# Stick attention with v as the stationary operand, memory projections spread between all heads, and the ends of the blocks in another order

## The chip, the cores and the metric

The kernel runs on one core of a Trainium2 chip as one launch. The metric is the device time of the launch in microseconds (us). TensorE (PE) multiplies, VectorE (DVE) and ScalarE (ACT) do the elementwise work, GpSimd (POOL) does almost nothing here, and SyncE (SP) starts the weight loads. Each engine runs its own list of instructions in order; semaphores order them against each other.

## What is computed

Two transformer blocks stand behind each other. The first one has a gated FFN, a mixer of two attentions, and a second gated FFN. The second one has two layers; this change concerns it above all:

```
# layer 0: latent attention (8 heads, a value width of 128)
lat = h @ w_dkv; c_q, c_kv = rmsnorm(lat[:384]), rmsnorm(lat[384:640])
q = c_q @ w_uq; k, v = c_kv @ w_ukv; softmax(q k^T + causal) v  @ w_o
# layer 1: stick attention (8 heads of 128)
z = q k^T * scale; log_fail = where(strict, -softplus(z), 0)
excl = cumsum(log_fail, reverse) - log_fail
a = where(strict, exp(log_sigmoid(z) + excl), 0);  o = a v  @ w_o
# after either: cross attention to 256 memory rows (4 heads), then square(relu(h w)) w
```

There are S = 256 rows of width 1024, kept as two tiles t of 128 rows. The memory's keys and values are `rmsnorm(mem) @ w_kv`; they do not depend on the layers before them.

## The kernel before

Every weight product is made three times, from float32r halves: `mm3` multiplies high by high, high by low, low by high (lines 377 to 379, of 512 columns mostly). The weights come as chunks of up to 4 tiles of 128x512, in the fixed order of `PLAN`. A chunk passes three stations: a load by SP into the ring `w_raw`, its high part by ACT (`split_hi`, L349), its low part by DVE (`split_lo`, L357). The ring has 4 slots. So where PE has finished chunk n, ACT and DVE split chunk n+4 (`next_hi`, `next_lo`). The place of `next_hi(n)` and `next_lo(n)` in the lists of ACT and DVE is written by hand in each phase. Whatever stands behind a split there waits for it.

Phases follow each other on each engine. What the prediction speaks of:

- `Ffn` steps. At a step, PE multiplies, ACT applies the activation (`take_up_scalar`, L653 or L656), DVE makes the product or the square (`hide_vector`, L715 or L719). At the end, `residual_vector` (L485) adds the result to h, in two halves of 512 columns; `norm_tensor` (L411) turns h on PE, `norm_scalar` (L421) and `norm_vector` (L467) take its high and low parts as `xt_h`, `xt_l`; `rms_scalar` (L430) and `root_vector` (L445 to L454) make the root mean squares, which are needed only where products are copied out of PSUM. `tail_scalar` and `tail_vector` set this order: three of the four splits, the first half of the norm, a split, the second half, and only then the phase `Norm` with the squares and the root.
- `Project` copies products out (`copy_out`, L927, with the row's factor from `rs`), turns them on PE (L884), and takes them. For 8x64 heads DVE makes a norm between (`squares`, L996; `normalise`, L1007). `mla_down` makes the two latents, `mla_up` multiplies them up.
- `Fill` is a projection of the memory, keys or values, in steps placed between the groups of an attention: 0 to 3 are 12 matmuls each, 2 and 7 also the splits, 4 the copy (L1144), 5 the turning and 6 the taking of keys (L1132, L1151).
- `Attend` for latent attention: in groups, scores (L1244), logits (L1339), exponential (L1319), turning of the probabilities (L1253), values (L1264); and `Finish`, which makes rows of the result (L1191), turns them (L1203) and takes them (L1210, L1216).
- `Stick`, one head at a time (g = 0 to 7): scores (L1546), mask on DVE (L1619), three functions on ACT (L1597 to L1599), softplus on DVE (L1629), suffix sums on PE (L1556 to L1558), their sum on DVE (L1625), the exponential on ACT (L1605), and the value product with the weights a as the stationary and v as the moving operand:

```
nc.tensor.matmul(bankD[0][g // 4][:, c], a[:, 0:P], vals[0], start=True, stop=True)
nc.tensor.matmul(bankD[1][g // 4][:, c], a[:, P:S], vals[0], start=True, stop=False)
nc.tensor.matmul(bankD[1][g // 4][:, c], a[:, S:S + P], vals[1], start=False,
                 stop=True).then_inc(self.summed, 1)
```

  This gives rows of o, so that `Finish` has to copy and turn them (L1197, L1203) before the output projection can use them. After every fourth head two tiles are finished.
- `OutProject` is the output projection; its tail is again `tail_scalar` and `tail_vector`.

## Time and profile before

| | before |
|---|---|
| median of 3 runs | 1339.06 us (1335.96 to 1339.08) |
| the profiled execution's own time | 1339.2 us |
| span of its trace | 1337.4 us |
| PE, DVE, ACT busy | 1277.5, 760.9, 649.4 us |
| mean granted TensorE clock | 0.992 |

The span runs from the first to the last instruction of the trace; 1.8 us of the time lie outside it. PE is busy for 96% of the span. Matmuls are pipelined and their ends are modelled, so an unbroken row of matmuls counts as busy throughout. A granted clock of 1.00 is 2.4 GHz, one of 0.50 is 1.2 GHz.

### The profile page before, as it was taken

Reading aid. Unit: us, or ns where it says so; the run is one execution under the profiler, and the core shown is the slowest. Engines: PE = TensorE matmul, PEld = TensorE weight load, DVE = VectorE, ACT = ScalarE, POOL = GpSimd, SP = SyncE. Lnnn points to the kernel's source line nnn. Section 1 sums busy time; section 2 is a strip of 40 time slices with the busy share of each in tenths; the row PEclk is TensorE's granted clock in tenths of the full one; section 3 lists DMA queues with packets and bytes.
Section 4 is the critical chain, followed back from the end, with each engine's and each line's share of the span. In section 5 each row is a group of like instructions: output and inputs, shape, how many; then the busy total and the mean of one; then the engine's idle time right before and its main releaser. Section 6 shows DMA issues by size and latency. Waiting matters only on the chain.

```text
span 1337.4 us, 16848 instructions
## 1 busy us (share of the span) xinstructions
PE 1277.5 (96%) x6786; PEld 1089.5 (81%) x6786; DVE 760.9 (57%) x1075; ACT 649.4 (49%) x828; POOL 11.9 (1%) x16
## 2 busy tenths in 40 slices
PE   6999998999999999997999999999999899999996
PEld 4888887888887888887888789999787777889895
DVE  6554448787675555547645475554644546654544
ACT  5444436464355454446844464443645645543432
POOL 0000000001000000000000000000000000000000
PEclk9999999999999999999999999999999899999998
DMA  6855545554444555545623265554554122555530
GB/s 248 283 188 188 187 142 209 189 173 134 166 148 149 185 188 187 189 137 171 210 73 111 79 235 185 184 190 144 212 188 169 69 95 88 208 197 190 188 124 32
DMA packets 38685, 221.72 MB, mean 166 GB/s; under 512 B 4533, under 2 KB 4549, under 8 KB 23120
## 3 DMA queue, kind: packets, MB, share of 16 engines
q1 hardware_dynamic: 36256, 214.26, 46.4%
q0 software_dynamic: 912, 3.75, 0.8%
q10 hardware_dynamic: 1440, 2.64, 0.8%
q8 instruction: 54, 0.88, 0.3%
q14 instruction: 23, 0.19, 0.0%
HBM read 219.55 MB, written 1.07 MB: 165 GB/s over the span
## 4 chain that ended last, share of the span: by engine, by line
PE 86%; DVE 6%; ACT 5%; issue 2%; DMA 1%; DVEq 0%; SPq 0%; ACTq 0%
PE ps L377 22%; PE ps L379 22%; PE ps L378 22%; PE ps L573 4%; PE ps L575 4%; PE ps L574 4%; DVE wlo L357 3%; PE ps L1244 2%; ACT whi L349 2%; PE ps L1264 2%; PE ps L411 1%; PE ps L884 1%; PE ps L1253 1%; PE ps L606 1%; ACT xt_h L421 1%
## 5 line engine op out<-in xcount | busy, mean ns | idle before, releaser
L357 DVE TENSOR_TENSOR wlo<-w_raw,whi 128x2048 fp32r<-128x2048 f32 (+4 forms) x245 | 470.2, 1924 | 415.9 <-ACT whi L349 415.5
L349 ACT ACTIVATE whi<-w_raw 128x2048 fp32r<-128x2048 f32 (+4 forms) x245 | 394.7, 1616 | 449.4 <-PE ps L379 344.5
L377 PE MATMUL ps<-whi,xt_h 128*128 128x512 f32 (+3 forms) x784 | 309.6, 395 | 11.6 <-DVE wlo L357 4.0
L379 PE MATMUL ps<-whi,xt_l 128*128 128x512 f32 (+3 forms) x784 | 304.2, 388 | 0.0
L378 PE MATMUL ps<-wlo,xt_h 128*128 128x512 f32 (+3 forms) x784 | 303.7, 387 | 0.0
L377 PE MATMUL ps<-whi,ot_h 128*128 128x512 f32 x594 | 235.9, 397 | 5.6 <-ACT nat L927 3.6
L379 PE MATMUL ps<-whi,ot_l 128*128 128x512 f32 x594 | 232.2, 391 | 0.0
L378 PE MATMUL ps<-wlo,ot_h 128*128 128x512 f32 x594 | 231.9, 390 | 0.0
L377 PEld LDWEIGHTS ps<-whi,xt_h 128*128 128x128 f32 x784 | 148.5, 189 | 46.4 <-issue 13.3
L379 PEld LDWEIGHTS ps<-whi,xt_l 128*128 128x128 f32 x784 | 148.3, 189 | 30.0
L378 PEld LDWEIGHTS ps<-wlo,xt_h 128*128 128x128 f32 x784 | 148.4, 189 | 27.5
L573 PE MATMUL ps<-xt_h,whi 128*128 128x256 f32 x512 | 145.3, 284 | 3.2 <-DVE xt_l L467 1.8
L574 PE MATMUL ps<-xt_h,wlo 128*128 128x256 f32 x512 | 144.9, 283 | 0.0
L575 PE MATMUL ps<-xt_l,whi 128*128 128x256 f32 x512 | 144.9, 283 | 0.0
L377 PEld LDWEIGHTS ps<-whi,ot_h 128*128 128x128 f32 x594 | 111.9, 188 | 28.8 <-issue 6.2
L379 PEld LDWEIGHTS ps<-whi,ot_l 128*128 128x128 f32 x594 | 111.8, 188 | 24.1
L378 PEld LDWEIGHTS ps<-wlo,ot_h 128*128 128x128 f32 x594 | 112.0, 189 | 21.7
L573 PEld LDWEIGHTS ps<-xt_h,whi 128*128 128x128 f32 x512 | 98.2, 192 | 4.9 <-issue 4.4
L574 PEld LDWEIGHTS ps<-xt_h,wlo 128*128 128x128 f32 x512 | 98.2, 192 | 0.5
L575 PEld LDWEIGHTS ps<-xt_l,whi 128*128 128x128 f32 x512 | 98.2, 192 | 0.0
L421 ACT ACTIVATE xt_h<-ps,gain 128x256 fp32r<-128x256 f32 x88 | 34.3, 479 | 49.4 <-PE ps L411 49.4
L467 DVE SCALAR_TENSOR_TENSOR xt_l<-ps,gain,xt_h 128x256 fp32r<-128x256 f32 x88 | 36.3, 477 | 23.0 <-ACT xt_h L421 23.0
(185 smaller groups left out, 871.6 us busy)
## 6 DMA issues: line engine op xcount, KB each, us to landing
w_raw<-ffn_mid SPq DMA_DIRECT2D x80, 768.0 KB, 4.3
w_raw<-mlp_mid SPq DMA_DIRECT2D x56, 1024.0 KB, 4.9
w_raw<-w_qkv SPq DMA_DIRECT2D x12, 1024.0 KB, 4.9
w_raw<-w_sb_qkv SPq DMA_DIRECT2D x12, 1024.0 KB, 4.8
w_raw<-w_xkv SPq DMA_DIRECT2D x8, 1024.0 KB, 4.8
w_raw<-ffn_first SPq DMA_DIRECT2D x8, 512.0 KB, 4.9
w_raw<-w_gate_b SPq DMA_DIRECT2D x4, 1024.0 KB, 5.0
w_raw<-w_gate_a SPq DMA_DIRECT2D x4, 1024.0 KB, 4.9
```

Of the source, the lines that this page charges most:

```text
L349: nc.scalar.activation(whi[:, s, 0:tiles * width], w_raw[:, s, 0:tiles * width], ACT.Copy).then_inc(w_hi, 1)
L357: nc.vector.tensor_tensor(wlo[:, s, 0:tiles * width], w_raw[:, s, 0:tiles * width], whi[:, s, 0:tiles * width].bitcast(F32), ALU.subtract) ...
L377: nc.tensor.matmul(acc, hi, whi[:, s, c], start=start, stop=False)
L378: nc.tensor.matmul(acc, hi, wlo[:, s, c], start=False, stop=False)
L379: return nc.tensor.matmul(acc, lo, whi[:, s, c], start=False, stop=stop)
L421: last = nc.scalar.activation(to[:, k], bank[:, j * S:(j + 1) * S], ACT.Copy, scale=gain[:, 8 * NORM[name] + k:8 * NORM[name] + k + 1])
L467: last = nc.vector.scalar_tensor_tensor(out=lo[:, k], in0=bank[:, j * S:(j + 1) * S], scalar=g, in1=hi[:, k].bitcast(F32), op0=ALU.mult, o ...
L573: nc.tensor.matmul(acc, whi[:, s, c], xt_h[:, k], start=k == 0, stop=False)
L574: nc.tensor.matmul(acc, wlo[:, s, c], xt_h[:, k], start=False, stop=False)
L575: last = nc.tensor.matmul(acc, whi[:, s, c], xt_l[:, k], start=False, stop=k == KC - 1)
L1244: last = nc.tensor.matmul(bankA[g % 2][:, head["at"]:head["at"] + head["width"]], q, k, start=i == 0, stop=i == len(head["qk"]) - 1)
L1264: last = nc.tensor.matmul(head["out"], pt[:, g % 2, c:c + P], val, start=i == 0, stop=i == len(head["v"]) - 1)
```

## The change

It has these parts, all of which leave the arithmetic as it is, except that the sums of some roots are made in two instructions' rows instead of one.

1. `Ffn`: at the start only one chunk is split ahead of the first activation instead of two. At the end DVE adds the residual first; the order is then a split, half of the norm, a split, the other half, squares and root, and then the last two splits.
2. `mla_down` and `mla_up`: the root for the query latent is made in a row of instructions of its own, ahead of the one for the key latent; `mla_up` waits for `mla_down`'s copies tile by tile.
3. Latent attention: heads are grouped in their own order, so that results can be finished after every fourth head. The memory's values come first and begin before the first scores (step -1); the keys come behind them, and their turning is placed in the output projection.
4. Stick attention: v is the stationary operand, so the result comes turned and goes from PSUM straight to `ot_h` and `ot_l`, a pair of heads at a time. There is no `Finish`. The memory's values, then its keys, stand between all heads.

```diff
-        for part in ("keys", "values"):
+        for part in ("values", "keys"):
             add(f"mem_{part}{i}", f"w_xkv{i}", [4] * 2)
...
@@ Ffn.scalar
-                for c in range(2):
-                    next_hi(act, self.n0 + c)
+                next_hi(act, self.n0)
                 act.wait_ge(rs_ready, RMS_AT[self.name])
                 self.take_up_scalar(act, 0)
-                for c in range(2, 4):
+                for c in range(1, 4):
                     next_hi(act, self.n0 + c)
...
-                tail_scalar(act, [self.n0 + 4 * self.steps + c for c in range(4)], self.following)
+                chunks = [self.n0 + 4 * self.steps + c for c in range(4)]
+                for half, n in enumerate(chunks[:2]):
+                    next_hi(act, n)
+                    if self.following:
+                        norm_scalar(act, self.following, half)
+                if self.following:
+                    rms_scalar(act, self.following)
+                for n in chunks[2:]:
+                    next_hi(act, n)
@@ Ffn.vector
-                for c in range(2):
-                    next_lo(dve, self.n0 + c)
+                next_lo(dve, self.n0)
                 self.hide_vector(dve, 0)
-                for c in range(2, 4):
+                for c in range(1, 4):
                     next_lo(dve, self.n0 + c)
...
+                for half, n in enumerate(chunks[:2]):
+                    residual_vector(dve, self.down_full, self.scale, half)
+                    next_lo(dve, n)
+                    if self.following:
+                        norm_vector(dve, self.following, half)
+                if self.following:
+                    root_vector(dve, self.following)
+                for n in chunks[2:]:
+                    next_lo(dve, n)
@@ Project
+                            if part and part[0] == unit.ks[0] and unit.u == 0 and self.before:
+                                pe.wait_ge(self.before.evac, NT * (len(self.before.units) - 1) + t + 1)
...
+                if unit.u == 3 and self.before:
+                    act.wait_ge(self.before.rooted, 2)
...
+            def root(self, dve, unit):
+
+                c = 2 * len(NORMS) + 2 * unit.u
+                dve.wait_ge(self.squared, unit.u + 1)
+                rsqrt(dve, ms[:, c:c + 2], rs[:, c:c + 2], 1.0, EPS, 2).then_inc(self.rooted, 1)
...
+                    if unit.kind == "latent":
+                        self.root(dve, unit)
...
@@ Attend.tensor and Stick.tensor
+                for filler, step in fill_steps(self.fillers, -1):
+                    filler.tensor(pe, step)
                 for s, value in self.need:
                     pe.wait_ge(s, value)
@@ Stick
+            def pair_bank(self, pair):
+                return bankD[0][pair % 2]
+
             def value(self, pe, g):
+
                 pe.wait_ge(self.weights, g + 1)
-                if g in self.bank_free:
-                    pe.wait_ge(*self.bank_free[g])
...
+                if g >= 4:
+                    pe.wait_ge(self.lo, g // 2 - 1)
...
-                nc.tensor.matmul(bankD[0][g // 4][:, c], a[:, 0:P], vals[0], start=True, stop=True)
-                nc.tensor.matmul(bankD[1][g // 4][:, c], a[:, P:S], vals[0], start=True, stop=False)
-                nc.tensor.matmul(bankD[1][g // 4][:, c], a[:, S:S + P], vals[1], start=False,
+                nc.tensor.matmul(bank[:, at:at + S], vals[0], a[:, 0:S], start=True, stop=False)
+                nc.tensor.matmul(bank[:, at + P:at + S], vals[1], a[:, S:S + P], start=False,
                                  stop=True).then_inc(self.summed, 1)
 
+            def take_hi(self, act, pair):
+                act.wait_ge(self.summed, 2 * pair + 2)
+                nc.scalar.activation(ot_h[:, 2 * pair:2 * pair + 2],
+                                     self.pair_bank(pair).rearrange("p (k s) -> p k s", k=2), ACT.Copy)\
+                    .then_inc(self.hi, 1)
...
@@ Stick.vector (Stick.scalar likewise)
                     for filler, step in fill_steps(self.fillers, g):
                         filler.vector(dve, step)
-                    for f in range(4):
-                        if self.fin.fins[f][2] == g - 1:
-                            self.fin.out_rows(dve, f)
-                        if self.fin.fins[f][2] == g - 2:
-                            self.fin.take_lo(dve, f)
+                    if g >= 3 and g % 2:
+                        self.take_lo(dve, g // 2 - 1)
@@ OutProject.tensor
+                    if c == 0 and self.aside:
+                        self.aside.tensor(pe, 5)
@@ mla_groups
-                for heads in same_half(per):
+                for heads in [list(range(h0, h0 + per)) for h0 in range(0, 8, per)]:
@@ the phases
+        values0 = memory_values(0, bankD[1], (-1, 0, 1, 2, 2, None, None, 3))
+        keys0 = memory_keys(0, bankD[0], [(rows_lo, rows0 + 1), (rows_lo, rows0 + 2)], 1,
+                            (4, 5, 6, 7, 7, None, None, 8), bankT)
...
+        values1 = memory_values(1, bankD[1], (-1, 0, 1, 2, 2, None, None, 3))
+        keys1 = memory_keys(1, bankD[1], [(fill_copied, values1.full0 + 1), (fill_copied, values1.full0 + 2)], 0,
+                            (3, 4, 5, 6, 6, 7, 7, 7))
+        stick = Stick("sb", [sb_in.turned_ready, sb_in.evac_ready], (values1, keys1))
+        sb_out = OutProject("sb_out", "sb_o", all8, ot_h, ot_l, [(stick.lo, 3), keys1.ready],
+                            following="cross1", need_k={6: (stick.lo, 4)})
```

The programs were laid beside each other at three places. The first is ACT's list at the end of the first FFN; L349 is a split, L421 (L419 after) the norm, L430 (L428) the squares, L927 (L944) the copy of the next phase's first product. Before:

```order
L349 ACTIVATE whi<-w_raw 128x2048 x2
L349 ACTIVATE whi<-w_raw 128x1296
L421 ACTIVATE xt_h<-ps,gain 128x256 x4
L349 ACTIVATE whi<-w_raw 128x1296
L421 ACTIVATE xt_h<-ps,gain 128x256 x4
L430 ACTIVATE lg,ms<-h 128x1024 x2
L349 ACTIVATE whi<-w_raw 128x2048
L927 ACTIVATE nat<-ps,rs 128x512 x2
```

And after:

```order
L349 ACTIVATE whi<-w_raw 128x2048
L419 ACTIVATE xt_h<-ps,gain 128x256 x4
L349 ACTIVATE whi<-w_raw 128x2048
L419 ACTIVATE xt_h<-ps,gain 128x256 x4
L428 ACTIVATE lg,ms<-h 128x1024 x2
L349 ACTIVATE whi<-w_raw 128x1296 x2
L349 ACTIVATE whi<-w_raw 128x2048
L944 ACTIVATE nat<-ps,rs 128x512 x2
```

Two splits have moved from ahead of the norm to behind the squares, so that three splits now stand between the squares and the first copy, where one stood. DVE's list has moved in the same way.

The second place is PE's list where latent attention begins, behind the last product of `mla_up`. Before:

```order
L378 MATMUL ps<-wlo,ot_h 128x512
L379 MATMUL ps<-whi,ot_l 128x512
L1244 MATMUL ps<-kt,qt 128x128
L1244 MATMUL ps<-pet 128x128
L1244 MATMUL ps<-kt,qt 128x128
```

And after:

```order
L378 MATMUL ps<-wlo,ot_h 128x512
L379 MATMUL ps<-whi,ot_l 128x512
L377 MATMUL ps<-whi,xt_h 128x512
L378 MATMUL ps<-wlo,xt_h 128x512
L379 MATMUL ps<-whi,xt_l 128x512
```

Twelve matmuls of the memory's values (the first three are shown) now stand ahead of the first scores.

The third place is DVE's list at the end of stick attention: L1619 (L1659 after) is the mask, L1625 (L1665) the sum of logits and suffix sums, L1629 (L1669) softplus, L1216 (L1609) the low part of the result. Before:

```order
L1619 TENSOR_TENSOR lg<-ps,const 128x384
L1625 TENSOR_TENSOR lg<-lg,ps 128x384
L1629 SCALAR_TENSOR_TENSOR pt<-lg,pt 128x384
L1625 TENSOR_TENSOR lg<-lg,ps 128x384
L357 TENSOR_TENSOR wlo<-w_raw,whi 128x2048
L1197 COPY nat<-ps 128x512 x2
L1216 TENSOR_TENSOR ot_l<-ps,ot_h 128x4x128 x2
```

And after:

```order
L1659 TENSOR_TENSOR lg<-ps,const 128x384
L1665 TENSOR_TENSOR lg<-lg,ps 128x384
L1669 SCALAR_TENSOR_TENSOR pt<-lg,pt 128x384
L357 TENSOR_TENSOR wlo<-w_raw,whi 128x2048
L1609 TENSOR_TENSOR ot_l<-ps,ot_h 128x512
L1665 TENSOR_TENSOR lg<-lg,ps 128x384
L1609 TENSOR_TENSOR ot_l<-ps,ot_h 128x512
```

The copies of rows are gone, and a split and a low part now stand ahead of the last head's sum, where they stood behind it.

## Rows read from the trace of the kernel before

**Rows 1.** The page: the engines' busy times; a weight load, its size and landing

```profile
PE 1277.5 (96%) x6786; PEld 1089.5 (81%) x6786; DVE 760.9 (57%) x1075; ACT 649.4 (49%) x828; POOL 11.9 (1%) x16
...
w_raw<-w_qkv SPq DMA_DIRECT2D x12, 1024.0 KB, 4.9
```

**Rows 2.** Stretches: length, busy PE, PEld, DVE, ACT, POOL, then PE's clock, DMA

```profile
66.80:100.20 33.40, 33.40 (x153) 27.64 (x152) 16.96 (x15) 14.77 (x14) 0.00 (x0) 1.00 0.56 188
...
199.00:231.00 32.00, 27.45 (x139) 22.89 (x138) 25.92 (x49) 21.16 (x29) 0.00 (x0) 0.95 0.54 188
422.00:435.00 13.00, 10.94 (x43) 8.59 (x42) 8.33 (x12) 7.82 (x8) 0.00 (x0) 0.87 0.62 207
600.00:634.20 34.20, 26.96 (x158) 24.19 (x157) 26.68 (x70) 23.83 (x48) 0.00 (x0) 1.00 0.54 181
658.50:709.00 50.50, 46.03 (x264) 39.14 (x264) 25.83 (x55) 25.38 (x53) 0.00 (x0) 1.00 0.35 122
946.00:970.00 24.00, 22.29 (x106) 18.03 (x105) 19.33 (x30) 15.96 (x19) 0.00 (x0) 1.00 0.65 233
1026.50:1084.00 57.50, 48.78 (x255) 40.63 (x254) 29.88 (x44) 33.98 (x54) 0.00 (x0) 0.94 0.24 85
```

**Rows 3.** PE at the first FFN's end: start, length, instruction, idle before

```profile
205.81 1.29 PE L411 MATMUL ps<-const,h 128*128 128x128 f32 x8 [2.96 <-DVE h L485]
```

**Rows 4.** DVE from there to the next phase's first norm

```profile
202.18 2.29 DVE L357 TENSOR_TENSOR wlo<-w_raw,whi 128x2048 fp32r<-128x2048 f32 x1 [1.95 <-ACT whi L349]
204.39 1.28 DVE L485 SCALAR_TENSOR_TENSOR h<-ps,h 128x512 f32<-128x512 f32 x2
...
217.53 0.17 DVE L445 TENSOR_SCALAR ms<-ms 128x2 f32<-128x2 f32 x1 [1.29 <-ACT lg L430]
...
229.78 1.29 DVE L1007 TENSOR_TENSOR nat<-nat,hs 128x512 f32<-128x512 f32 x2
```

**Rows 5.** ACT over the same stretch

```profile
217.41 1.90 ACT L349 ACTIVATE whi<-w_raw 128x2048 fp32r<-128x2048 f32 x1
221.33 0.69 ACT L927 ACTIVATE nat<-ps,rs 128x512 f32<-128x512 f32 x1 [2.02 <-PE ps L379]
```

**Rows 6.** The starts of the FFNs: PE in the first, DVE and PE in the second

```profile
29.98 0.47 PE L377 MATMUL ps<-whi,xt_h 128*128 128x512 f32 x1 [1.07 <-DVE nat L715]
...
423.42 3.43 DVE L357 TENSOR_TENSOR wlo<-w_raw,whi 128x1536 fp32r<-128x1536 f32 x2 [0.53 <-ACT whi L349]
426.77 0.87 DVE L715 SCALAR_TENSOR_TENSOR nat<-ps,rs,lg 128x256 f32<-128x256 f32 x2
...
427.39 0.47 PE L377 MATMUL ps<-whi,xt_h 128*128 128x512 f32 x1 [2.06 <-DVE nat L715]
```

**Rows 7.** PE in the latent projections

```profile
626.25 0.47 PE L377 MATMUL ps<-whi,ot_h 128*128 128x512 f32 x1 [0.88 <-ACT nat L927]
...
633.97 0.47 PE L377 MATMUL ps<-whi,ot_h 128*128 128x512 f32 x1 [2.71 <-ACT nat L927]
```

**Rows 8.** PE in latent attention: its start, and the output projection's start

```profile
661.37 0.46 PE L1244 MATMUL ps<-kt,qt 128*128 128x128 f32 x2 [1.50 <-ACT v L918]
...
708.60 0.47 PE L377 MATMUL ps<-whi,ot_h 128*128 128x512 f32 x1 [0.82 <-issue]
```

**Rows 9.** ACT behind the first MLP: the stick projection's first copy

```profile
965.71 0.69 ACT L927 ACTIVATE nat<-ps,rs 128x512 f32<-128x512 f32 x1 [1.74 <-PE ps L379]
```

**Rows 10.** Stick attention: PE after head 3 and at the end, then ACT

```profile
1058.93 1.46 PE L1203 MATMUL ps<-const,nat 128*128 128x128 f32 x8 [2.73 <-DVE nat L1197]
...
1078.22 1.25 PE L1203 MATMUL ps<-const,nat 128*128 128x128 f32 x8 [1.55 <-DVE nat L1197]
...
1083.05 0.47 PE L377 MATMUL ps<-whi,ot_h 128*128 128x512 f32 x1 [0.82 <-issue]
...
1059.97 0.52 ACT L1597 ACTIVATE pt<-lg 128x384 f32<-128x384 f32 x1 [4.02 <-DVE lg L1619]
...
1061.60 0.51 ACT L1605 ACTIVATE nat<-lg 128x384 f32<-128x384 f32 x1
```

More of the change, by code:

```diff
@@ L382, in norm_banks @@
         def norm_banks(name):
[L385 removed]
+            if name.startswith("mem"):
                 return bankD[1] + bankD[0]
[L387 to L388 removed]
             return bankT + bankD[0]
@@ L1114, in tensor @@
                         pe.wait_ge(xt_lo, 4 * NORM[self.normed] + 2 * (c + 1))
-                    if step == 0:
-                        for s, value in self.free:
+                    if c == 0:
+                        for s, value in self.free[t:t + 1]:
                             pe.wait_ge(s, value)
@@ L1575, in tensor @@
                 self.score(pe, 0)
-                for g in range(H2 + 3):
+                for g in range(H2 + 1):
                     if g + 1 < H2:
```

119 lines of the change are left out of this document (59 added, 60 removed).

## The prediction

> **What bounds the kernel.** I read the page first. PE is busy for 1277.5 of 1337.4 us, the others for 57% and less [rows 1]. In a dense stretch it has no gap: 153 matmuls in 33.40 us, 0.22 each [rows 2]. So an edit pays only by removing PE work or PE's waits, 59.9 us in all. The stretches that the change touches hold half of the waits: length less PE's busy time is 4.55, 2.06, 7.24, 4.47, 1.71 and 8.72 us, 28.8 together [rows 2]. The rest is in the start, the cross attentions and the end, which stay. In three of those stretches the clock was also granted at half rate for a while: a mean of 0.95 over 32 us is 3.2 us at 1.2 GHz, 0.87 over 13 is 3.4, 0.94 over 57.5 is 6.9 [rows 2]. A 3.4 us spell costs 1.7 us of dense work. Such spells came in the stretches with waits of 2.96, 2.06 and 2.73 us [rows 3, 6, 10], none in the one with a wait of 2.71 [rows 2, 7].
>
> My method is to carry the new order through: each instruction keeps its duration from the trace and starts when its engine is free and its inputs are there. What counts is by how much PE's next unavoidable point comes earlier, not the wait that is removed.
>
> **Starts of the FFNs.** PE waits 1.07 us for the product of step 0 [rows 6]; and since a matmul behind a wait counts 0.47 long [rows 6] where the pace is 0.22 [rows 2], a wait also costs part of that difference, for which I take 0.16. With one split ahead instead of two the product comes 1.7 earlier, half of the pair that takes 3.43 [rows 6]: the first FFN gains 1.2. In the second, ACT's activation then starts as soon as the product of tile 0 is full, DVE's split ends at 425.1, its product at 425.5, and PE goes on at 425.6 instead of 427.39 [rows 6]: 1.75, and the half-clock spell should go with the wait, 1.7 more. Cover for the split that is now later: the first chunk of the step, 18 matmuls or about 4 us, against 3.1 for its two parts. In the MLPs nothing is gained: there DVE's root ends after the activation, and the first split stands behind it in either order.
>
> **End of the first FFN.** DVE splits (202.18, 2.29) before it adds the residual (204.39), and PE waits 2.96 until 205.81 [rows 3, 4]. PE stopped at 202.85, one chunk of 6 matmuls beyond what the residual needs. So in the new order the residual can start at about 201.0 and ends at 202.3, before PE gets there, and PE turns h at once and begins the next projection at 205.3, 4.9 earlier. But two splits now stand behind the squares. ACT: squares end at 212.4 (217.4 less 5.0), two splits of 1296 columns (1.2 each) and one of 2048 (1.9) follow, and the copy that stood at 221.33 [rows 5] starts at 216.7; PE wants it at 217.05, a wait of 0.3. DVE: root at 212.5 (217.53 less 5.0); from there to the normalise it took 12.25, of which 0.33 idle [rows 4], and two splits of 1.4 come in between: 227.3 instead of 229.78, only 2.5 earlier. PE reaches the turn that needs it at 224.5 and waits 3.4. So the gain is 2.5, and a wait of 3.4 us on DVE's L1007 stands where the one on L485 stood. It is longer than the one that brought the clock down before, so I charge 1.7 for a spell.
>
> **End of the second FFN and the latents.** The same way PE begins `mla_down` 3.8 earlier. Three splits ahead of the first copy give 1.7 back as a wait. Then the root of the query latent, a row of twelve small instructions that starts with one like that of 217.53 [rows 4] and takes 2.3 in the trace, stands ahead of DVE's `lower` and `rotate`: `mla_up` starts at 624.75 instead of 626.25, with a wait of 2.2 in place of 0.88 [rows 7]. The wait of 2.71 for the copy behind it [rows 7] is not ended by the root at all: ACT first takes the key latent, which PE has just turned, and that order stays. It moves with PE, to 2.9. Net gain 1.6.
>
> **Latent attention.** The values' first 12 matmuls (2.7 us) cover the wait of 1.50 for the last copy of v; the output projection no longer waits 0.82 for the copy of the bank [rows 8], since a bank is copied while the other one fills; the finishes (the rest of the 4.47 [rows 2]) now have a fill step behind each. Followed through, one wait of 0.35 stays, at the second finish. PE's work is the same: 96 fill matmuls, the same scores, turns and values. Gain 4.1, and 0.16 for each of five waits: 5.0.
>
> **End of the first MLP.** PE begins the stick projection 1.9 earlier. But ACT's squares, moved by as much, end at 960.1, three splits of 1.9 follow, and the copy of 965.71 [rows 9] comes at 965.8 all the same. PE waits 1.7 and the gain is 0.2.
>
> **Stick attention.** The value product keeps its 384 moving columns per head (three matmuls of 128 before, one of 256 and one of 128 now). What goes are 16 transposes, 8 of them in 1.46 at half clock or 0.87 at full [rows 10], so 1.7 us, and the waits for the copied rows, 2.73 and 1.55 [rows 10]. The start gains nothing: the first values step waits about 1.5 for `xt_l`, which the scores used to cover, and the first softplus is late anyway, because DVE's last split of the projection stands ahead of the first mask. Through head 2 all stays. Then splits (DVE 2.29, ACT 1.90 [rows 4, 5]) stand in the steps of heads 3, 5 and 7, each followed by a pair's two parts (0.6 and 0.65), and behind them the next mask, three functions (1.64 from 1059.97 to 1061.60 [rows 10]) and softplus. I get the suffix products of heads 4, 6 and 7 at 1056.0, 1066.5 and 1069.9, with waits of 0.7 to 1.0. The last head is the sore point: DVE's sum for it now stands behind a split and a low part. ACT takes the keys and splits until 1072.6, DVE until 1075.4, the sum ends at 1075.9, the exponential at 1076.5, while PE is done with head 6 at 1071.4: a wait of 5.1 us in front of the last value product. The output projection starts at 1077.25 instead of 1083.05 [rows 10]: gain 5.8. One spell behind the 5.1 us wait costs 1.7; the 6.9 us of before are in the 1083.05 already.
>
> **Sum.** 1.2 + 3.5 + 2.5 + 1.6 + 5.0 + 0.2 + 5.8 = 19.8, less 3.4 for two spells, 16.4. From the profiled execution's 1339.2, which is the median of the runs within 0.2, this gives 1322.8.
>
> **A rule weighed.** The trace shows spells in the stretches of the waits of 2.96, 2.06 and 2.73, but a clock of 1.00 through the one with 2.71 and 0.88 [rows 2, 7]. The Trainium skill, in TensorE: Matmul & The Clock Gate, section What's actually happening, says that the low rate is the default and activity lifts it; by that rule each of my new waits may bring a spell, and the time would be that of the third case below.
>
> **Rivals.**
> 1. As worked out: 1318 to 1327, chance 0.50.
> 2. The splits aren't in the way as I think, because the engines catch up. Then the ends of the three blocks give 4.9, 4.0 and 1.9 instead of 2.5, 1.6 and 0.2 (6.5 more), the 5.1 wait goes and both spells (3.4): 15 more, 1308. Range 1303 to 1318. Against it: DVE was idle for only 6.1 us of the 32 at the first FFN's end [rows 2]. Chance 0.16.
> 3. The clock falls more often: the two new waits of 2.2 and 2.9 in the latents bring a spell each and stick attention a second one, 1.7 each: 1328. Up to 1332. For it: the 6.9 us behind one wait of 2.73. Chance 0.20.
> 4. The attentions aren't shortened. They alternate between four engines, and if each hand-over takes the slack, 5.0 and 5.8 shrink to the transposes' 1.7: 1332. For it: DVE and ACT were idle for nearly half of these stretches (29.88 and 33.98 busy of 57.5 [rows 2]), so it is latency that sets them; against it: PE had work in most gaps. Chance 0.08.
> 5. Slower. Two splits later at three block ends also means that the loads into their slots start later, since SP waits for both parts of the split. If the weights of four chunks later came late, PE would stand. At the first FFN's end the split ends at 216.4 instead of 209.3; the load (4.9 [rows 1]) and the next split (1.9 and 2.3) end at 226, and PE wants that chunk behind two more products, after 239. It decides only if loads take 13 us longer, and for a slower kernel 5.5 us more at each of three places. Chance 0.04.
>
> The remaining 0.02 is for gains and losses that cancel. A measurement of this kernel tells 0.3%, some 4 us, from no change. Cases 1 to 4 all end below 1335: faster 0.94, same 0.02, slower 0.04. The range 1312 to 1332 leaves out the better half of case 2 and the tails of 3 and 4, about 2 in 10.
>
> **What would show it.** In the new profile: no PE wait on the residual at the ends of the FFNs; instead waits of about 3.4 on the normalise, 1.7 on the first copies, 2.2 and 2.9 in the latents; 0.3 at the second FFN's start with the clock at 1.00; at most 0.5 of waits in latent attention; one wait of about 5 in front of the last head's values. If PE's busy time falls by more than the 2 us of the transposes and the spells, I have misread the swap. The likeliest error is in the waits of a few us that I worked out over chains of ten or more instructions.

## The result and the profile after

The changed kernel took 1324.18 us (median of 4 runs, 1322.03 to 1325.89) and the kernel before, measured beside it, 1337.53. The ratio is 0.9892, with a 95% interval from 0.9867 to 0.9917. A second measurement gave 1323.26 us and a ratio of 0.9894 [0.9881, 0.9908]. The gain is real, about 14 us by the ratios and 13.3 by the medians, where the forecast had 16.4. The time of 1324.2 lies 1.4 above the forecast of 1322.8.

The page of the changed kernel, PE's line, answers to [rows 1]:

```profile
PE 1273.8 (96%) x6754; PEld 1088.0 (82%) x6754; DVE 760.2 (57%) x1083; ACT 648.3 (49%) x828; POOL 11.9 (1%) x16
```

The span fell from 1337.4 to 1324.1 us, 13.3. PE's busy time fell by 3.7, so waits of PE make up the other 9.6. The same stretches as in [rows 2], moved by about as much as PE came earlier there (columns: stretch, length, busy PE, PEld, DVE, ACT, POOL, clock, DMA):

```profile
198.00:227.90 29.90, 26.38 (x141) 22.39 (x140) 26.26 (x49) 22.25 (x30) 0.00 (x0) 0.99 0.58 204
418.40:429.80 11.40, 11.01 (x51) 8.81 (x50) 9.05 (x18) 9.58 (x11) 0.00 (x0) 1.00 0.34 107
592.70:630.90 38.20, 32.12 (x173) 28.49 (x172) 29.61 (x84) 26.11 (x50) 0.00 (x0) 0.95 0.48 162
655.20:700.10 44.90, 43.95 (x257) 38.37 (x256) 25.23 (x54) 22.99 (x49) 0.00 (x0) 1.00 0.39 133
...
1017.80:1069.20 51.40, 43.73 (x221) 36.14 (x220) 28.80 (x40) 34.29 (x54) 0.00 (x0) 0.98 0.32 113
```

Length less busy PE is the waits: 0.39 at the second FFN's start (2.06 before), 0.95 in latent attention (4.47 before), but 7.67 in stick attention (8.72 before), and 6.08 in the latents. So stick attention got shorter by 6.1 us with only 1.05 us less of waits in it; what fell there is PE's busy time, by 5.05. About 2 us of that is the clock and not work: the half-clock spell of before, 6.8 us long, lies in its stretch whole, while the new one starts at 1067.2 and this stretch ends at 1069.2. The 16 transposes were 2.3 us: from their first start to the start of what follows, eight took 1.25 from 1058.93 on and eight 1.01 from 1078.22 on.

PE's own rows say which waits those are. They are nearly the new ones of the forecast:

```profile
29.02 0.47 PE L377 MATMUL ps<-whi,xt_h 128*128 128x512 f32 x1
...
227.05 1.72 PE L899 MATMUL ps<-const,nat 128*128 128x128 f32 x8 [3.15 <-DVE nat L1024]
228.42 0.78 PE L377 MATMUL ps<-whi,xt_h 128*128 128x512 f32 x1
...
423.82 0.47 PE L377 MATMUL ps<-whi,xt_h 128*128 128x512 f32 x1 [0.39 <-DVE nat L721]
...
610.00 0.38 PE L377 MATMUL ps<-whi,xt_h 128*128 128x320 f32 x1 [1.46 <-ACT nat L944]
619.74 0.53 PE L377 MATMUL ps<-whi,ot_h 128*128 128x512 f32 x1 [1.80 <-DVE ot_l L1066]
629.10 0.47 PE L377 MATMUL ps<-whi,ot_h 128*128 128x512 f32 x1 [2.71 <-ACT nat L944]
...
682.16 0.66 PE L1227 MATMUL ps<-const,nat 128*128 128x128 f32 x4 [0.95 <-DVE nat L1215]
...
958.01 0.47 PE L377 MATMUL ps<-whi,xt_h 128*128 128x512 f32 x1 [1.31 <-ACT nat L944]
...
1019.50 0.50 PE L377 MATMUL ps<-whi,xt_h 128*128 128x512 f32 x1 [1.46 <-DVE xt_l L465]
1026.96 0.70 PE L1581 MATMUL ps<-pt,const 128*128 128x256 f32 x2 [0.36 <-DVE pt L1669]
...
1067.06 1.09 PE L1597 MATMUL ps<-nat,v 128*128 128x256 f32 x2 [4.74 <-ACT nat L1646]
1067.94 0.63 PE L1598 MATMUL ps<-nat,v 128*128 128x128 f32 x2
1068.23 0.77 PE L377 MATMUL ps<-whi,ot_h 128*128 128x512 f32 x1
1068.80 0.63 PE L378 MATMUL ps<-wlo,ot_h 128*128 128x512 f32 x1
```

A spell here is a stretch in which the granted clock is 0.50. A matmul of 512 columns in an unbroken row shows 0.63 us there instead of 0.4. The trace's clock record has four spells of 3.4 us each ahead of the last ten us in the changed kernel, at 227.5, 620.1, 630.3 and 1067.2 us, at most 1.2 us behind the ends of the waits of 3.15, 1.80, 2.71 and 4.74. Before it had three, at 206.5, 428.4 and (6.8 us, twice as long as each of the others) 1059.8. The profiled execution of the changed kernel is the slowest of its four (1325.89 us).

By how much does the same matmul of PE come earlier? The table takes the matmul of the same ordinal at each place. "Behind the spell" is a matmul a few us later, where a spell that one of the two kernels has there is over.

| place | before | after | earlier by |
|---|---|---|---|
| first FFN, step 0's product | 29.98 | 29.02 | 0.96 |
| behind the turn of the normed heads | 231.54 | 228.42 | 3.12, and 1.96 behind the spell at 227.5 |
| second FFN, step 0's product | 427.39 | 423.82 | 3.57, and 5.15 behind before's spell |
| `mla_up` | 626.25 | 619.74 | 6.51, and 3.29 behind the spells at 620.1 and 630.3 |
| latent attention's output projection | 708.60 | 699.70 | 8.90, soon 8.11 |
| stick projection, behind its first wait | 966.81 | 958.01 | 8.80 |
| stick attention's output projection | 1083.05 | 1068.23 | 14.82, and 13.70 behind the spell at 1067.2 |
| end of the span | 1337.4 | 1324.1 | 13.3 |

### The profile page after: what moved, and what is told of

It is laid out like the page before. It is cut to its first block, busy times and chain, and to the rows that moved or that the text cites. A ratio compares the mean times of both kernels' runs of the same rounds, so it can differ in the third digit from the quotient of the medians.

```text
span 1324.1 us, 16795 instructions
## 1 busy us (share of the span) xinstructions
PE 1273.8 (96%) x6754; PEld 1088.0 (82%) x6754; DVE 760.2 (57%) x1083; ACT 648.3 (49%) x828; POOL 11.9 (1%) x16
## 3 DMA queue, kind: packets, MB, share of 16 engines
HBM read 219.55 MB, written 1.07 MB: 167 GB/s over the span
## 4 chain that ended last, share of the span: by engine, by line
PE 86%; DVE 7%; ACT 5%; issue 2%; DMA 0%; DVEq 0%; SPq 0%; ACTq 0%
PE ps L377 22%; PE ps L379 22%; PE ps L378 22%; PE ps L572 4%; PE ps L574 4%; PE ps L573 4%; DVE wlo L357 3%; PE ps L1268 2%; PE ps L1288 2%; ACT whi L349 2%; PE ps L899 1%; PE ps L409 1%; PE ps L1277 1%; ACT xt_h L419 1%; PE ps L605 1%
## 5 line engine op out<-in xcount | busy, mean ns | idle before, releaser
L349 ACT ACTIVATE whi<-w_raw 128x2048 fp32r<-128x2048 f32 (+4 forms) x245 | 394.5, 1616 | 433.6 <-PE ps L379 329.7
L419 ACT ACTIVATE xt_h<-ps,gain 128x256 fp32r<-128x256 f32 x88 | 34.3, 479 | 52.1 <-PE ps L409 52.1
```

The lines of the kernel that those rows point to most:

```text
L349: nc.scalar.activation(whi[:, s, 0:tiles * width], w_raw[:, s, 0:tiles * width], ACT.Copy).then_inc(w_hi, 1)
L419: last = nc.scalar.activation(to[:, k], bank[:, j * S:(j + 1) * S], ACT.Copy, scale=gain[:, 8 * NORM[name] + k:8 * NORM[name] + k + 1])
```

## The experiments

All ratios are to the kernel before, each measured beside it on the same chip; the kernel before took 1338.5 to 1338.7 us there. Gains in us are worked out from the ratios.

**The same kernel again.** Nothing is edited; its profile shows the same instructions a second time.

> The changed kernel once more, as the reference for the runs beside it. 0.989 of the kernel before, about 1324 us; half-clock spells at other places than before are likely, each worth 1.7 us.

It took 1323.26 us (1322.56 to 1325.87), 0.9894 [0.9881, 0.9908]. The waits are the same, the clock isn't. Its stretches:

```profile
198.00:229.50 31.50, 27.98 (x144) 24.02 (x143) 28.40 (x50) 23.04 (x30) 0.00 (x0) 0.95 0.62 217
592.70:627.50 34.80, 28.72 (x166) 25.84 (x165) 28.82 (x83) 25.22 (x49) 0.00 (x0) 1.00 0.53 178
1017.80:1069.20 51.40, 45.21 (x219) 37.42 (x218) 26.16 (x33) 30.21 (x47) 0.00 (x0) 0.93 0.29 103
```

and PE's rows in the latents:

```profile
618.63 0.50 PE L377 MATMUL ps<-whi,ot_h 128*128 128x512 f32 x1 [1.80 <-DVE ot_l L1066]
626.38 0.47 PE L377 MATMUL ps<-whi,ot_h 128*128 128x512 f32 x1 [2.71 <-ACT nat L944]
```

The waits of 1.80 and 2.71 are there again, yet the latents ran at a clock of 1.00, with no spell, where the first profile had two; between the two rows lie 7.75 us here and 9.36 there. In stick attention it is the other way round: the spell behind the last values' wait is 6.8 us long here (from 1062.1) and 3.4 in the first profile. The means of 0.93 and 0.98 exaggerate this, as the stretch ends inside the first profile's spell. Against [rows 7], PE is here at both rows 7.6 us earlier than before; in the first profile it was 6.51 and then 4.87 earlier. So the spells of this stretch come in one execution of a kernel and not in another, and cost what a row of dense matmuls loses at half the clock. Those behind the waits of 3.15 and 4.74 are in both profiles (here at 225.9 and 1062.1).

**FFN starts alone.** The kernel before with only this edit, and the same on DVE:

```diff
-                for c in range(2):
-                    next_hi(act, self.n0 + c)
+                next_hi(act, self.n0)
                 act.wait_ge(rs_ready, RMS_AT[self.name])
                 self.take_up_scalar(act, 0)
-                for c in range(2, 4):
+                for c in range(1, 4):
```

> The kernel before with one edit alone: at the start of each FFN one chunk is split ahead of the first activation instead of two. My theory: PE's wait of 1.07 us in the first FFN goes, the one of 2.06 in the second shrinks to about 0.4 and the half-clock spell behind it (1.7 us) goes, the MLPs stay as they are; 4.7 us less than before, about 1333. Rival: the spell stays somewhere else, then 3.0 less. Rival: the later splits are missed by PE a chunk later, then no gain at all.

1336.46 us against 1338.69, ratio 0.9980 [0.9970, 0.9991], which is 2.7 us less: the first rival, not the 4.7 of the theory. The wait of 1.07 is gone, that of 2.06 is 0.39, and the stretch has its full clock:

```profile
420.00:433.00 13.00, 12.61 (x58) 10.11 (x57) 10.23 (x19) 10.45 (x11) 0.00 (x0) 1.00 0.41 130
598.00:637.40 39.40, 33.43 (x176) 29.11 (x175) 27.51 (x71) 24.92 (x50) 0.00 (x0) 0.91 0.52 174
```

But the latents, untouched, ran at 0.91 here and at 1.00 before [rows 2]. This profile has spells at 205.6 (6.8 us), 601.5 and 632.3 that the profile before does not have, or has at half the length, and it is of the slowest of 11 executions (1338.39 us, clock 0.989; the fastest had 1333.76 and 0.993). Over the 11 the mean granted clock is 0.9914, over the 22 of the kernel before 0.9918, so on the whole the 1.7 for the spell that the edit removes was paid again elsewhere. The waits' 2.7 to 3.0 us are what the edit is sure of.

**The ends undone.** The changed kernel with the old order at the ends of the FFNs and of the first MLP (residual behind the third split, the squares and the root in a phase of their own):

```diff
-                chunks = [self.n0 + 4 * self.steps + c for c in range(4)]
-                for half, n in enumerate(chunks[:2]):
-                    residual_vector(dve, self.down_full, self.scale, half)
-                    next_lo(dve, n)
...
+                tail_vector(dve, [self.n0 + 4 * self.steps + c for c in range(4)], self.following,
+                            self.down_full, self.scale)
```

> The changed kernel with the old order at the ends of the FFNs (three splits, norm, split, norm, then squares and root); all else as changed. My theory: the ends gave only 2.5 + 1.6 + 0.2 = 4.3 us in waits and cost half-clock spells in return (three of them, 227.5, 620.1 and 630.3, stand in the changed kernel's trace, one at 206.5 in that of before), so that undoing them costs between 0 and 3 us: 1324 to 1327. PE should wait about 3 us on the residual at the first FFN's end again, and not on L1024. Rival: the ends gave what their removed waits promise, 4.9 + 4.0 + 1.9 = 10.8 us; then about 1335.

1326.96 us, 0.9917 [0.9900, 0.9935]; the changed kernel's ratio is 0.9892 to 0.9894, so the new ends are worth about 3 us. That is at the upper end of what was expected, and the intervals overlap a little. PE's rows at the first FFN's end:

```profile
204.81 1.06 PE L409 MATMUL ps<-const,h 128*128 128x128 f32 x8 [2.96 <-DVE h L483]
209.21 0.47 PE L377 MATMUL ps<-whi,xt_h 128*128 128x512 f32 x1 [1.94 <-DVE xt_l L465]
231.05 1.15 PE L883 MATMUL ps<-const,nat 128*128 128x128 f32 x7 [1.02 <-DVE nat L1008]
```

5.9 us of waits here, against 0.29 (on `xt_l`) and 3.15 in the changed kernel. The difference of 2.5 us is as large as the gain that the prediction worked out for this end.

**Stick part alone.** The kernel before with the new `Stick` and, in layer 1, the values and then the keys between all heads:

```diff
-        stick = Stick("sb", [sb_in.turned_ready, sb_in.evac_ready], fills1, {4: fills1[0].ready})
-        sb_out = OutProject("sb_out", "sb_o", all8, ot_h, ot_l, [stick.ready, fills1[1].ready],
-                            following="cross1")
+        stick = Stick("sb", [sb_in.turned_ready, sb_in.evac_ready], (values1, keys1))
+        sb_out = OutProject("sb_out", "sb_o", all8, ot_h, ot_l, [(stick.lo, 3), keys1.ready],
+                            following="cross1", need_k={6: (stick.lo, 4)})
```

> The kernel before with the stick part alone: v stationary, result taken in pairs straight from PSUM, the memory's values and keys of the second layer in the new places. My theory: the output projection behind stick attention starts 5.8 us earlier relative to its start, one half-clock spell behind the wait of about 4.7 in front of the last values costs 1.6 of it: 4.2 less than before, about 1333.3. Rival: the swap pays by its matmuls and transposes alone, 1.7 us. Rival: no spell, 5.8 less.

1334.98 us, 0.9976 [0.9966, 0.9986], 3.2 us less by the ratio, where 4.2 were expected. The wait in front of the last values is there (4.73 us at 1077.13, L1571 on ACT's L1620).

**The swap without the new places.** The same, but with the memory's keys in the steps of heads 0 to 5 and its values behind head 6, as before:

```diff
-                       (-1, 0, 1, 2, 2, None, None, 3))
...
-                     lambda t: nat[:, 0, t], [], row("mem0"), (3, 4, 5, 6, 6, 7, 7, 7), rel[:, 0:4])
+        keys1 = Fill("mem_keys1", bankD[1], [], lambda t: nat[:, 0, t], [(mem_root.rooted, 1)], row("mem0"),
+                     (0, 0, 1, 2, 2, 3, 3, 5), rel[:, 0:4])
...
+                       lambda t: mem_v[:, t], [], row("mem0"), (7, 8, 9, 10, 11, None, None, 11))
```

> The kernel before with v as the stationary operand in stick attention and the pairs' copies to ot_h and ot_l, but with the memory's keys and then its values where they stood: keys in the steps of heads 0 to 5, values behind head 6, so the values' products cover the end of the last heads. My theory: the swap takes away the rows' copies with the waits of 2.73 and 1.55 in front of their turning, and 1.7 of transposes, and leaves waits on softplus in the heads without a fill; together about 5, so 1332 to 1335 where the kernel before takes 1338.7, as much as the stick part with moved fills gave. Rival A, the new places of the fills are what counts and the swap gives only the transposes: 1337. Rival B, the moved fills cost more (the split ahead of the last sum) than they give: then this kernel is clearly better than the stick part with moved fills, at 1331 or less.

1338.05 us against 1338.47, 0.9994 [0.9986, 1.0003]: nothing that can be told. My theory (about 5 us) was wrong, and rival B too; rival A, the places count, comes nearest in time, though not even the 1.7 of the transposes is left. Two things took the gain back, longer waits and the clock. PE's rows:

```profile
1034.80 0.70 PE L1555 MATMUL ps<-pt,const 128*128 128x256 f32 x2 [1.71 <-DVE pt L1643]
1052.49 1.22 PE L1555 MATMUL ps<-pt,const 128*128 128x256 f32 x2 [2.46 <-DVE pt L1643]
1063.31 1.22 PE L1555 MATMUL ps<-pt,const 128*128 128x256 f32 x2 [4.69 <-DVE pt L1643]
```

and DVE's ahead of the third:

```profile
1057.55 2.29 DVE L357 TENSOR_TENSOR wlo<-w_raw,whi 128x2048 fp32r<-128x2048 f32 x1 [1.92 <-ACT whi L349]
1059.76 0.68 DVE L1583 TENSOR_TENSOR ot_l<-ps,ot_h 128x512 fp32r<-128x512 f32 x1
1060.36 0.55 DVE L1633 TENSOR_TENSOR lg<-ps,const 128x384 f32<-128x384 f32 x1
1060.83 0.55 DVE L1639 TENSOR_TENSOR lg<-lg,ps 128x384 f32<-128x384 f32 x1
1062.70 0.56 DVE L1643 SCALAR_TENSOR_TENSOR pt<-lg,pt 128x384 f32<-128x384 f32 x1 [1.33 <-ACT pt L1614]
```

The waits of 2.73 and 1.55 on the copied rows are gone, and the softplus waits took their place: 2.46 where there had been 0.64 and less, and 4.69 where there had been 0.68, because the next head's mask (L1633) stands behind a split (2.29) and a low part, and ACT's three functions and the softplus come behind the mask. (Ahead of the 2.46 it stands behind a low part alone, which waited 1.41 for its high part.) All six waits of stick attention together were 7.7 us before (1.71, 0.64, 0.37, 2.73, 0.68, 1.55) and are 8.9 here, so 1.2 us of what the transposes gave is lost again. It is the chain of one head that sets the pace at these places, mask to functions to softplus to suffix sums, and part of the time for turning the rows had only filled it.

The other part is the clock. Stick attention's stretch shows

```profile
1020.00:1083.50 63.50, 53.54 (x258) 44.86 (x257) 29.50 (x41) 37.78 (x59) 0.00 (x0) 0.92 0.26 91
```

which is 10.2 us at half the clock, in two spells that start within the waits of 2.46 and 4.69, where the kernel before has 6.8. It is not only this profile: the mean granted clock of the 11 executions is 0.9907 (0.989 to 0.994), that of the 15 of the kernel before 0.9921, and 0.0014 of 1337 us are 1.9 us. So at an equal clock the swap would have given about 2.3 to 2.7 us, an estimate from these means and the 0.4 to 0.8 us of the times. With the new places of the memory's products (the stick part alone) the mean granted clock is 0.9916 again.

**Both attention parts alone.** The kernel before with both attention parts and the separate root for the query latent, without the starts and ends of the FFNs:

> The kernel before with both attention parts and the separate root of the query latent, without the new starts and ends of the FFNs. My theory: 4.8 from latent attention and about 3.7 to 6 from stick attention, as far as a half-clock spell takes some of it back: 1328 to 1330 where the kernel before takes 1338.7. Rival, the attentions give back what they gain and the ends of the blocks make most of the change's gain: 1333 or more.

1330.12 us against 1338.47, 0.9941 [0.9929, 0.9954], 7.9 us less. Of these the stick part is 3.2, so 4.7 are left for latent attention and the root, where the table above has 4.8. Its own profile agrees: against the kernel before, PE is 0.1 us later at the first matmul of `mla_up` (626.35 for 626.25) and 4.7 earlier behind latent attention (709.48 for 714.16). The three groups of parts alone give 2.7, 3 and 7.9, together 13.6 of the 14.2 to 14.4 of the whole change.

**No fill ahead of the first scores.** One number of the changed kernel:

```diff
-        values0 = memory_values(0, bankD[1], (-1, 0, 1, 2, 2, None, None, 3))
+        values0 = memory_values(0, bankD[1], (0, 0, 1, 2, 2, None, None, 3))
```

> The changed kernel, but in latent attention the first step of the memory's values stands behind the first scores, not ahead of them. In the trace of before PE waited 1.50 there for the last copy of v. My theory, that this step covers that wait: about 1.5 longer than the changed kernel, 1325 to 1326 against 1323.3 to 1324.2, and the wait of 1.5 is back in PE's rows. Rival, the slack moves on: the step is then missing ahead of the scores but covers a wait of the same size a group later, and the time stays within 0.5.

1324.23 us, 0.9902 [0.9886, 0.9918]. The time can't tell 1.5 from nothing: the ratios differ by 0.0008 to 0.001, about 1.2 us, and the intervals overlap. The profile can:

```profile
656.68 0.46 PE L1268 MATMUL ps<-kt,qt 128*128 128x128 f32 x2 [1.50 <-ACT v L935]
682.51 0.65 PE L1227 MATMUL ps<-const,nat 128*128 128x128 f32 x4 [0.95 <-DVE nat L1215]
```

The wait of 1.50 of before is back, and the next one, 0.95, is what it is in the changed kernel, so nothing later was covered in its stead. Laid beside the first profile of the changed kernel, PE is 1.40 us earlier at the end of `mla_up` (a spell less there) and 0.36 later at the first matmul of `mla_out`, with no spell between. So latent attention takes 1.76 us longer without the early step, and the rival is out.

**The last sum ahead of the last split.** The 4.74 us wait was worked out as DVE's sum standing behind a split. The edit puts that split, of the keys' second chunk, behind the last head:

```diff
-                            (3, 4, 5, 6, 6, 7, 7, 7))
+                            (3, 4, 5, 6, 6, 7, 7, 8))
```

> The changed kernel with one number changed: the last split of the memory's keys in stick attention stands in step 8 instead of 7, so that DVE makes the last head's sum ahead of that split. My theory: the wait of 4.74 us in front of the last values is the split on ACT (1.9) and the one on DVE (2.3) less what overlaps; it shrinks to about 1.5, a gain of 3.2, and the half-clock spell behind it goes too, 1.6 more: about 1319.5. Rival: the split only moves in front of the output projection's own second chunk, and the gain is given back: 1324. Rival: the spell comes anyway: 1321.

1316.83 us, 0.9843 [0.9827, 0.9859], some 6.6 us less than the changed kernel, where 4.8 were expected. DVE in the changed kernel:

```profile
1063.09 2.29 DVE L357 TENSOR_TENSOR wlo<-w_raw,whi 128x2048 fp32r<-128x2048 f32 x1 [2.62 <-ACT whi L349]
1065.30 0.68 DVE L1609 TENSOR_TENSOR ot_l<-ps,ot_h 128x512 fp32r<-128x512 f32 x1
1065.90 0.55 DVE L1665 TENSOR_TENSOR lg<-lg,ps 128x384 f32<-128x384 f32 x1
```

and in this one:

```profile
1057.70 0.69 DVE L1609 TENSOR_TENSOR ot_l<-ps,ot_h 128x512 fp32r<-128x512 f32 x1 [1.31 <-ACT ot_h L1603]
1058.31 0.54 DVE L1665 TENSOR_TENSOR lg<-lg,ps 128x384 f32<-128x384 f32 x1
1061.24 2.29 DVE L357 TENSOR_TENSOR wlo<-w_raw,whi 128x2048 fp32r<-128x2048 f32 x1 [2.39 <-ACT whi L349]
```

PE's wait there:

```profile
1059.46 0.70 PE L1597 MATMUL ps<-nat,v 128*128 128x256 f32 x2 [1.22 <-ACT nat L1646]
```

The wait fell by 3.5. The clock record has no spell at this place any more: 3.4 us at half the clock in the first profile of the changed kernel, 6.8 in the second. Against the second, which has the same clock up to here, PE is 3.5 us earlier at this matmul and 6.3 behind the spell. So a little over half of the 6.6 is the wait and the rest is the clock.

**First copy and normalise ahead of the splits, and the latents.** Two edits of the changed kernel, each alone. The first puts, in a projection's first unit, ACT's copy ahead of the split that stood before it, and DVE's normalise ahead of the last split:

```diff
+                    if first:
+                        next_lo(dve, unit.n[0][0])
+                        self.normalise(dve, unit)
...
-                    if unit.kind == "qk":
+                    if unit.kind == "qk" and not first:
```

> The changed kernel, with the first copy of the phase behind an FFN ahead of ACT's third split, and on DVE, behind the first FFN, the squares ahead of the splits of the next product's two chunks and the normalise ahead of the second of them. My theory: the wait of 3.15 us on the normalise shrinks to about 1.2, the 1.31 at the stick projection and most of the 1.46 in the latents go; the second of these only moves into the wait behind it. 2 + 1.4 = 3.4 us less than the changed kernel, and the half-clock spell behind the 3.15 may go (1.7 more): 1319 to 1321. Rival: the splits are late for PE in their new place (at the second chunk of the next product), and nothing is gained.

1318.89 us, 0.9855 [0.9837, 0.9873], 5.2 less than the changed kernel. PE's row at the first FFN's end:

```profile
224.71 1.26 PE L899 MATMUL ps<-const,nat 128*128 128x128 f32 x8 [1.28 <-DVE nat L1029]
```

The wait on the normalise is 1.28 instead of 3.15 and no spell follows it. The first copy's 1.31 at the stick projection is gone. In the latents its 1.46 became one of 1.02 on a split's low part, and 2.71 stands in front of `mla_up` where 1.80 did. The second edit makes the root of the query latent behind DVE's `lower`, and ACT takes the last latent behind the first copy of `mla_up`:

```diff
                     if before is not None and before.kind in ("latent", "dkv"):
                         self.lower(dve, before)
+                    if before is not None and before.kind == "latent":
+                        self.root(dve, before)
...
+                    if unit.u == 0 and self.before:
+                        self.before.take(act, self.before.units[-1])
```

> The changed kernel, with the root of the query latent behind its lower part on DVE, and the first copy of the up projection ahead of the taking of the key latent on ACT. My theory: the wait of 1.80 on the lower part becomes a few tenths, the one of 2.71 on the copy goes: 4.3 us less, and the two half-clock spells around them (620.1 and 630.3) go as well, 3.4 more: 1316.5 to 1320. Rival: the copy itself has then to wait for the root, so that only one of the two waits pays: 1321.5. Rival: spells come elsewhere: 1320.

1319.15 us, 0.9855 [0.9841, 0.9868], 5.2 less as well. The wait of 2.71 is gone, the 1.80 is 0.82, and its profile has no spell in the latents:

```profile
618.10 0.50 PE L377 MATMUL ps<-whi,ot_h 128*128 128x512 f32 x1 [0.82 <-DVE ot_l L1068]
```

**All three together.** The last three edits in one kernel:

> The changed kernel with the three edits together: the last head's sum ahead of the last split, the first copies ahead of the third split, and the order in the latents. My theory: the waits that go are different ones and add up: 3.5 + 3.4 + 4.3 = 11 us, and of the four half-clock spells inside the changed kernel at most one stays, up to 5 more: 1309 to 1313. Rival: the engines behind are the bound and each edit uses the same slack; then about 1316, as with the best of the three alone.

1310.00 us (1308.18 to 1310.21), 0.9785 [0.9772, 0.9798]: 28.7 us less than the kernel before, twice what the change brought. By the ratios the three edits alone give 6.6, 5.2 and 5.2, and 14.6 together, 2.4 less than their sum. Its own page has PE busy for 1267.6 of 1308.1 us. Its stretches (end of the first FFN, latents, stick attention):

```profile
198.00:226.00 28.00, 26.43 (x144) 22.75 (x144) 24.93 (x48) 21.85 (x29) 0.00 (x0) 1.00 0.55 189
590.00:625.00 35.00, 31.86 (x174) 28.41 (x173) 28.77 (x83) 25.34 (x50) 0.00 (x0) 0.95 0.52 177
1010.00:1057.00 47.00, 44.35 (x228) 36.87 (x227) 26.08 (x34) 31.20 (x48) 0.00 (x0) 1.00 0.26 90
```

The waits are 1.6, 3.1 and 2.7 us there (the last stretch leaves out the wait of 1.46 on `xt_l` at 1008.7; with it 4.1, against 7.67 in the changed kernel), and only the latents still have a spell.

## Why the prediction was right, and where it was off

**Direction, size and places** were right. The waits came where they were put, and nearly as long: 3.15 on the normalise (3.4 worked out), 0.39 at the second FFN's start (0.3), 1.46 and 1.31 on first copies (1.7 each), 1.80 and 2.71 in the latents (2.2 and 2.9), 1.46 on `xt_l` (1.5), 4.74 in front of the last values (5.1). Smaller than said were the softplus waits of heads 4, 6 and 7, 0.41, 0.09 and 0.51 (0.7 to 1.0), and longer was that in latent attention, 0.95 (0.35), beyond the 0.5 that was given as the most. Nearly all the lengths were worked out 0.2 to 0.4 too long. A chain carried through by hand with whole durations errs this way, since neighbours overlap a little: DVE's split of 2.29 that starts at 1063.09 has a successor at 1065.30, 0.08 before its counted end. That such overlaps over ten or more steps are the whole of the error is argued from this one and not shown.

**The terms**, from the table above (spells included where they fall):

| term | predicted | measured |
|---|---|---|
| start of the first FFN | 1.2 | 0.96 |
| end of the first FFN, less its spell | 2.5 - 1.7 | 1.0 |
| start of the second FFN, with its spell | 3.5 | 3.2 |
| end of the second FFN, latents | 1.6 | -1.9 |
| latent attention | 5.0 | 4.8 |
| end of the first MLP | 0.2 | 0.6 |
| stick attention | 5.8 | 6.0 |
| behind the last values' wait, to the end | -1.7 | -1.5 |
| sum | 16.4 | 13.2 |

One term is off by much. The latents were predicted at 1.6 and came to -1.9, and the difference of 3.5 is two spells behind the waits of 1.80 and 2.71, 1.7 each. That is two of rival 3's three spells. In the second profile the latents have no spell, and PE there was 7.6 earlier than before, 1.3 more than behind the start of the second FFN, so that the term is 1.3 there for the 1.6 predicted. So the mechanism of the term was right, and whether those spells are charged is decided anew in each execution. The 1.4 us between forecast and median are less than the 3.9 between the fastest and the slowest of the four runs. That they are so few is in part luck: the forecast took its 16.4 from 1339.2, an execution 1.7 slower than the median of the kernel before beside the changed one.

**Stick attention** came out right in its sum (6.0 for 5.8), but its reading was too kind to the swap. The prediction credited the transposes (1.7) and the waits of 2.73 and 1.55 to the swap. Alone it brought 0.4 to 0.8 us, as waits of 1.2 more and some 1.9 of half clock took the rest. With the new places of the memory's products the part brought 3.2 us, and the ill placed split still held back 6.6 more, as the experiment with that split behind the last head shows. Of the 6.0 about 2.6 is the clock: some 6.1 us of PE's matmuls ran at half the clock in the stretch before, which costs 3.1, and 1.0 us ahead of the output projection after.

**Readings and sums.** The prediction took eight transposes for 1.46 us at half the clock and 0.87 at full. The row of 1.46 starts 0.9 us ahead of the spell at 1059.8, and from start to next start the two rows took 1.25 and 1.01, so what went is 2.3 us, not 1.7. In latent attention 4.1 and five times 0.16 make 4.9, not 5.0. PE's busy time fell by 3.7, more than the 2 us that the prediction had named as the sign of a misread swap. The transposes are 2.3 of it. An estimate of the rest: PE has 32 idle stretches of over 0.05 us where it had 40, and each of the 8 that went was priced at 0.16, which gives 1.3. So the sign pointed at waits that went and at transposes priced too low, and not at the value product.

**The rule weighed.** Of the waits that the changed kernel has, those of 3.15 and 4.74 us brought the clock to half in both profiles. Those of 1.80 and 2.71 did in one and not in the other. The Trainium skill, in TensorE: Matmul & The Clock Gate, section What's actually happening, says of a kernel's start that the number of matmuls at the low rate varies from run to run. These two profiles, with four spells and two behind the same waits, vary in the midst of a kernel too.

**The rivals.** Rival 1 was it. Rival 2 (no splits in the way, 1308) failed: the waits came, and the kernel with three edits more shows what they cost, since it takes the splits out of the way at three places and gets to 1310. Rival 3 was right in the first profile for the two spells of the latents, and in the second for the one of double length in stick attention, but never for all three. Rival 4 (attentions not shortened) is out by the 7.9 us of the two parts alone. Rival 5, late loads: PE's longest wait on a split in the changed kernel is the one of 4.0 us that stood before too. The list of waits after (total us, how many, longest):

```profile
PE ps L409 <- DMA gain<-gains: 7.3, 1, 7.3
PE ps L377 <- ACT nat L944: 5.5, 3, 2.7
PE ps L1597 <- ACT nat L1646: 4.7, 1, 4.7
PE ps L377 <- DVE wlo L357: 4.0, 1, 4.0
PE ps L899 <- DVE nat L1024: 3.1, 1, 3.1
```

**What stays open.** The fill ahead of the first scores is worth 1.76 us in the profiles, but the times of the launch can't tell it. The new places of the memory's products without the swap weren't tried, so the share of the two in the 3.2 us is known only from the one side. Of the 4.7 of latent attention only the early fill was taken apart; the grouping of heads, the separate root and the turning of the keys in the output projection were not.

## What to carry to other kernels

Where engines run lists in order, ask of each dependent short instruction what long and independent one stands ahead of it: one number in a table, moving a split of 2.29 us behind a sum of 0.55, gave 6.6 us, half as much as the whole change: 3.5 of wait, the rest half-clock time that followed it. A wait that is taken away is worth what the next chain leaves of it: carry the order through to PE's next unavoidable point, as the end of the first FFN (wait of 2.96 gone, one of 3.15 new, 2.5 gained) and the swap (waits of 2.73 and 1.55 gone, 2.46 and 4.69 new) show. Operations taken out of a loop whose pace is set by a chain across engines leave holes, and here the holes brought more half-clock time too; put new work there.

## What the hardware showed that I had not expected

The same waits cost different times in two executions of one kernel. The changed kernel's profiles have four half-clock spells and two (the second of double length, 6.8 us) ahead of the last ten us, with waits equal to 0.01 to 0.02 us at 1.80, 2.71 and 4.74, and its runs spread over 1322.0 to 1325.9. An edit that shortens one wait (the FFN starts alone) had a spell less there and two more in the latents, some 175 and 205 us later.

All thirteen profiles together show how far the length of the wait tells it. A wait counts as having brought a spell where one starts in it or up to 1.6 us behind it. The first 20 us of the launch are left out, as the clock record starts behind them.

| wait of PE, us | profiles that have it | with a spell |
|---|---|---|
| 4.7 (last values, or softplus in the swap alone) | 9 | 9 |
| 3.15 (normalise) | 5 | 5 |
| 2.96 (residual, end of the first FFN) | 6 | 5 |
| 2.73 (turned rows in stick attention) | 2 | 2 |
| 2.71 (second wait of `mla_up`) | 11 | 4 |
| 2.06 (start of the second FFN) | 4 | 3 |
| 2.0 (end of the second FFN) | 6 | 1 |
| 1.80 (first wait of `mla_up`) | 4 | 2 |

So a spell is a charge that a wait of about 2 to 3 us may bring and that the waits of 3.15 and 4.7 always brought here, of 1.7 us in dense work, or 3.4 where it is of double length. For a small edit it is the waits that should be counted, and the clock left out of the sum or put into the range. The mean granted clock over all executions of both kernels shows afterwards how much of a difference is the clock, as with the swap alone.
